# Four modulation units of layer 1 inside attention's last quarter, and experts 0 to 3 loaded ahead of the first gather

## What is computed

```python
def _ada(cond, w_ada, b_ada):
    m = (jax.nn.silu(cond) @ w_ada + b_ada)[..., None, :]
    return jnp.split(m, N_MOD, axis=-1)

for i in range(DEPTH):                      # once for the context, once for the latent tokens
    sh_a, sc_a, g_a, sh_f, sc_f, g_f = _ada(c, w_ada[i], b_ada[i])
    h = _modulate(x, sh_a, sc_a)            # layernorm(x) * (1 + scale) + shift
    ...                                     # attention (i = 0) or Fourier mixing (i = 1) -> out
    x = _post_norm(x, g_a * out, ln_gain[i, 0], ln_bias[i, 0])
    h = _modulate(x, sh_f, sc_f)
    moe = _hier_moe(h, ...)                 # top-1 group, top-2 experts in it, gated MLP
    x = _post_norm(x, g_f * moe, ln_gain[i, 1], ln_bias[i, 1])
```

## Time and profile before

| | |
|---|---|
| median of 3 runs | 989.13 us (987.59 to 990.61) |
| the profiled execution | 989.98 us, span in the trace 988.2 us |
| TensorE busy (matmuls) | 833.8 us, 84% |
| VectorE busy | 342.2 us, 35% |
| HBM read | 313.62 MB; mean 328 GB/s over the span |
| chain that ended last | TensorE 47%, DMA 32%, VectorE 13% |
| `DMA ring<-in_w_expert_up` in it | 17% |
| layer 0: first gather, first gate/up | 317.64 us, 326.94 us |

### The profile page before, as it was taken

The page is one execution under the profiler, slowest core; times in us unless marked ns, Lnnn a source line. Parts: engine busy times, 40 slices in busy tenths (PEclk is TensorE's granted clock), DMA queues, the critical chain, the costliest instruction groups (busy, mean ns, idle before and its releaser), DMA issues.

```text
span 988.2 us, 12750 instructions
## 1 busy us (share of the span) xinstructions
PE 833.8 (84%) x4891; PEld 428.5 (43%) x4891; DVE 342.2 (35%) x832; ACT 140.3 (14%) x327; POOL 164.5 (17%) x250
## 2 busy tenths in 40 slices
PE   3889999998898798998888788999599978786954
PEld 3555666665458333333333335547333323332311
DVE  2113454555587111111111138568511110111146
ACT  0122222223110111111101012001111100110110
POOL 1041212123111211111111100131201111111000
PEclk9989999999996999999899999998599998999978
DMA  9997393438449897999999979968999999999951
GB/s 335 366 358 289 114 380 126 170 131 324 156 126 415 353 402 285 420 420 418 419 419 418 417 284 370 350 234 298 351 383 419 418 419 418 419 420 419 417 194 64
DMA packets 91756, 324.54 MB, mean 328 GB/s; under 512 B 12654, under 2 KB 25678, under 8 KB 67608
## 3 DMA queue, kind: packets, MB, share of 16 engines
q1 hardware_dynamic: 73936, 287.84, 74.1%
q0 software_dynamic: 12704, 21.86, 6.3%
q10 hardware_dynamic: 5032, 13.71, 3.5%
HBM read 313.62 MB, written 32.05 MB: 350 GB/s over the span
## 4 chain that ended last, share of the span: by engine, by line
PE 47%; DMA 32%; DVE 13%; issue 4%; ACT 2%; POOL 2%; SPq 1%; POOLq 0%; ACTq 0%; DVEq 0%
DMA ring<-in_w_expert_up 17%; PE psum L1028 15%; PE psum L908 8%; DMA h_hT<-in_w_expert_up 5%; PE psum L1050 5%; PE psum L804 4%; PE psum L880 3%; DMA arena<-h_scratch,gidx 3%; PE psum L855 3%; DMA ring<-in_w_ada 3%; PE psum L1012 2%; DMA y_scratch<-arena,sidx 2%; DMA m_scratch<-m 1%; DMA ring<-y_scratch 1%; PE psum L959 1%
## 5 line engine op out<-in xcount | busy, mean ns | idle before, releaser
L1028 PE MATMUL psum<-ring,arena 128*64 128x512 f32 x880 | 260.3, 638 | 35.4 <-DMA ring<-in_w_expert_up 26.2
L1028 PEld LDWEIGHTS psum<-ring,arena 128*64 128x64 f32 x880 | 86.5, 146 | 168.9 <-issue 165.7
L1050 PE MATMUL psum<-ring,arena 128*64 128x512 f32 x440 | 124.1, 598 | 20.2 <-DVE arena L1809 19.6
L1805 DVE TENSOR_TENSOR arena<-arena,psum 128x256 f32<-128x256 f32 x34 | 14.3, 420 | 283.7 <-ACT arena L1363 283.7
L1028 PE MATMUL psum<-h_hT,arena 128*64 128x512 f32 x208 | 96.2, 617 | 7.2 <-DMA ring<-in_w_expert_up 6.3
L908 PE MATMUL psum<-ring,h_hT 128*128 128x384 f32 x288 | 98.1, 494 | 0.0
L855 PE MATMUL psum<-ring,h_hT 128*128 128x512 f32 x160 | 69.3, 593 | 1.8 <-ACT h_hT L1448 1.5
L908 PEld LDWEIGHTS psum<-ring,h_hT 128*128 128x128 f32 x288 | 54.4, 194 | 35.0 <-issue 1.6
L664 POOL DMA_INDIRECT y_scratch<-arena,sidx x32 | 32.6, 1019 | 208.4 <-DVE arena L1815 208.4
L804 PE MATMUL psum<-ring,silu 128*32 128x128 f32 x1536 | 55.2, 306 | 14.0 <-DMA ring<-in_w_ada 14.0
L1050 PEld LDWEIGHTS psum<-ring,arena 128*64 128x64 f32 x440 | 35.6, 136 | 71.6 <-issue 46.9
(11 more groups left out here) (215 smaller groups left out, 884.3 us busy)
## 6 DMA issues: line engine op xcount, KB each, us to landing
ring<-in_w_expert_down SPq DMA_DIRECT2D x52, 1024.0 KB, 21.4
ring<-in_w_expert_gate SPq DMA_DIRECT2D x50, 1024.0 KB, 19.0
ring<-in_w_expert_up SPq DMA_DIRECT2D x50, 1024.0 KB, 22.0
ring<-in_w_ada SPq DMA_DIRECT2D x24, 2048.0 KB, 14.6
h_hT<-in_w_expert_gate SPq DMA_DIRECT2D x12, 1024.0 KB
h_hT<-in_w_expert_up SPq DMA_DIRECT2D x12, 1024.0 KB
h_hT<-in_w_expert_down SPq DMA_DIRECT2D x12, 1024.0 KB, 26.6
ring<-in_w_qkv SPq DMA_DIRECT2D x9, 1024.0 KB, 12.6
```

The lines of the kernel that those rows point to most:

```text
L1028: last = pe.matmul(bank[b][64 * e:64 * e + 64, :].rearrange("p (g n) -> p g n", g=2), mem.GT[b][:, c, 64 * e:64 * e + 64], w, start=(c == ...
L1050: last = pe.matmul(bank[5 + half][64 * e:64 * e + 64, :], mem.actT[b][:, f, 64 * e:64 * e + 64], w[:, f, 512 * half:512 * half + 512], sta ...
```

## The change

Units (1, 2) and (1, 3) move from behind the router into attention's quarter 4, which now holds four units at the steps 1, 3, 4 and 5 (two before, at 1 and 4). They share a bank region, so each waits for VectorE's read of the one before. Unit (1, 5) moves from behind the table matmuls to behind (1, 4) and the router. Places change: units 4 and 5 now use C1 and A2, so A0 and A1 are free once attention's output is projected. SyncE loads expert 0 behind unit (1, 2); expert 2 and the gate part of expert 3 when that projection is done (where units 4 and 5 were loaded); expert 1 after unit (1, 4); the up and down parts of expert 3 after unit (1, 5). Experts 2 and 3 no longer wait for the first gathers; expert 4 does, as before. Nothing is computed that wasn't before, and nothing is left out.

```diff
-BETWEEN = {1: [(0, 4), (0, 5), (0, 6)], 2: [(0, 7), (0, 8), (0, 9)], 3: [(0, 10), (0, 11)], 4: [(1, 0), (1, 1)]}
-SPOTS = {1: (1, 3, 5), 2: (1, 3, 5), 3: (1, 4), 4: (1, 4)}
+BETWEEN = {1: [(0, 4), (0, 5), (0, 6)], 2: [(0, 7), (0, 8), (0, 9)], 3: [(0, 10), (0, 11)],
+           4: [(1, 0), (1, 1), (1, 2), (1, 3)]}
+SPOTS = {1: (1, 3, 5), 2: (1, 3, 5), 3: (1, 4), 4: (1, 3, 4, 5)}
...
-PLACE.update({("ada", 1, u): place for u, place in enumerate(("A2", "C1", "A2", "C1", "A0", "A1"))})
+PLACE.update({("ada", 1, u): place for u, place in enumerate(("A2", "C1", "A2", "C1", "C1", "A2"))})
...
-        ADA_AFTER = {(0, 1): (0, 2), (0, 3): (0, 1), (1, 1): (1, 0)}
+        ADA_AFTER = {(0, 1): (0, 2), (0, 3): (0, 1), (1, 1): (1, 0), (1, 2): (1, 1), (1, 3): (1, 2)}
...
             load("ada", 1, 0)
-            sp.wait_ge(qkv_ps, 18)
-            load_expert(0, 0)
             sp.wait_ge(qkv_ps, 24)
             load("ada", 1, 1)
-            for u in (2, 3):
-                after_ada(1, u - 2)
-                load("ada", 1, u)
+            after_ada(1, 0)
+            load("ada", 1, 2)
+            load_expert(0, 0)
+            after_ada(1, 1)
+            load("ada", 1, 3)
+            after_ada(1, 2)
+            load("ada", 1, 5)
+            after_ada(1, 3)
+            load("ada", 1, 4)
             sp.wait_ge(proj_ps, 6)
-            for u in (4, 5):
-                load("ada", 1, u)
-            after_ada(1, 3)
+            load_expert(0, 2)
+            load_part(0, 3, 0, "w_expert_gate")
+            after_ada(1, 4)
             load_expert(0, 1)
             after_ada(1, 5)
-            first_rows_fetched(0)
-            for e in (2, 3):
-                load_expert(0, e)
+            load_part(0, 3, 1, "w_expert_up")
+            load_down(0, 3)
             load_last_slot(0)
...
-                for u in ((2, 3, 4), (10,))[l]:
+                for u in ((4, 5), (10,))[l]:
                     ada(1, u)
...
-                if l == 0:
-                    ada(1, 5)
                 pe.wait_ge(table_done, 3 * l + 3)
...
-                for u in (range(2, 6), (11, 10))[l]:
+                for u in ((4, 5), (11, 10))[l]:
                     ada_add(1, u)
```

More of the change, by code:

```diff
@@ L388, in ada_out @@
             else:
-                at = [(4, 0), (4, 0), (1, 1), (1, 2), (1, 3), (7, 0), (2, 0), (5, 0), (5, 0), (3, 0), (1, 1), (1, 2)][u]
+                at = [(4, 0), (4, 0), (4, 0), (4, 0), (1, 1), (1, 2), (2, 0), (5, 0), (5, 0), (3, 0), (1, 1), (1, 2)][u]
             return bank[at[0]][:, P * at[1]:P * at[1] + P]
-        ADA_AFTER = {(0, 1): (0, 2), (0, 3): (0, 1), (1, 1): (1, 0)}
+        ADA_AFTER = {(0, 1): (0, 2), (0, 3): (0, 1), (1, 1): (1, 0), (1, 2): (1, 1), (1, 3): (1, 2)}
         ADA_AFTER.update({(0, u): (0, u - 1) for u in range(4, ADA_UNITS)})
@@ L421, in load_gate_up, with load_part @@
                 for part, name in enumerate(("w_expert_gate", "w_expert_up")):
-                    sp.dma_start(mem.slot(e)[:, part * 2 * D:(part + 1) * 2 * D],
-                                 A[name][l][e].rearrange("(p k) n -> p (k n)", p=P)).then_inc(landed[SLOT_OF[e]], 16)
+                    load_part(l, e, part, name)
+            def load_part(l, e, part, name):
+                sp.dma_start(mem.slot(e)[:, part * 2 * D:(part + 1) * 2 * D],
+                             A[name][l][e].rearrange("(p k) n -> p (k n)", p=P)).then_inc(landed[SLOT_OF[e]], 16)
             def load_down(l, e):
```

## The result

The changed kernel takes 1001.77 us (median of 4 runs, 1000.22 to 1003.87) against 988.84 us (987.59 to 990.61) for before: ratio 1.0126, 95% interval 1.0101 to 1.0151. It is slower, as forecast, but by 12.9 us and not by 7.25: it lies 1.3 us above the range. The profiled execution took 1000.94 us, its span is 999.1 us. In `mixer_to_experts` and behind, lines on TensorE are numbered 8 higher than before, those on VectorE 6 higher.

What follows compares the result with a forecast made beforehand. TensorE was taken to set the pace to 392 us, transfers to bound layer 0's experts after; 4.8 - 0.3 + 0.8 + 0.55 + 1.4 = +7.25 us on 989.13 gave 996.4 us, range 990.5 to 1000.5.

Steps and rivals of the forecast that it cites:

- first gather: First gather of layer 0's experts: lands later because the DMA queue drains 2.1 MB later; +1.4 us, bounds 0 and 3.0.
- unit at s = 3: Attention's quarter 4: the unit ahead of head 2's projection counts whole, since TensorE has no idle time there; +1.9 us.
- wait for unit 3's weights: Quarter 4, step 5: unit 3's load stands behind expert 0 and lands late; +2.1 us, bounds 0 and 5.5.
- unit at s = 5 and the head behind it: Quarter 4, ahead of head 4's projection: a 1.9 us unit, 1.07 us hidden by VectorE's softmax difference; +0.8 us.
- routing: Behind the router two units instead of three, but VectorE's one-hot sum sets the start of the position matmuls; -0.3 us.
- transposes: First transposes of gathered rows in layer 0, at clock 0.50 once the unit before them is gone; +0.8 us.
- gate/up of pair 0: Layer 0's first gate/up, slower at the low clock; +0.55 us, the middle of bounds 0 and 1.1.
- Head start worth nothing: Loading experts 2 and 3 ahead, 15.7 us of transfer, only lengthens idle DMA time before 393 us; 0 us gain.
- rival of 980.7 us: Rival: the 15.7 us of transfer done early shorten layer 0's transfer-bound stretch, giving 980.7 us; chance 0.07.
- Nothing behind absorbs it: After the first gate/up the whole +7.25 us remains: TensorE paces to 392 us, transfers take the same 168 us.
- a case to which the forecast gave 0.04: Rival: VectorE or DMA waits set the projection stage's end and swallow the delay; 989 to 991 us, chance 0.04.
- all upper bounds: Rival: wait 5.5, gather 3.0 and gate/up 1.1 all at their upper bounds; +12.8, 1002 us, chance 0.08.

Runs made afterwards that it cites:

- second profile of the changed kernel: The changed kernel measured and profiled once more with no edit, against before: 1004.43 us, ratio 1.0160.
- the kernel of both late: The changed kernel with expert 0 loaded behind unit 3's weights and experts 2 and 3 after the first gathers: 990.12 us, 1.0016 of before.

## Why the prediction was wrong in size

For the units and for the lost head start the mechanism held. The step that failed is the price of the early loads: 0 for the head start and +1.4 us for the first gather, where the stores and the gather beside them, and the clock behind the gather, cost about 10 us. It was hidden in part by an error the other way: the kernel with the units moved and the loads late is 1.0028 of before, 2.8 us, and not the 5.85 us that the sum has without the gather. The second failed step is that a wait of TensorE was priced at its own length. By the forecast's own steps, in the changed kernel's profile against that of before:

| step | forecast | measured |
|---|---|---|
| unit at s = 3 | +1.9 | +1.9 |
| wait for unit 3's weights | +2.1 (0 to 5.5) | +3.7 (3.41 idle) |
| unit at s = 5 and the head behind it | +0.8 | +2.85 |
| last head of quarter 4, low clock | not seen | +1.4 |
| routing | -0.3 | -1.1 |
| stores late, so the first gather issued late | not seen | +2.8 |
| first gather | +1.4 | +1.4 |
| transposes | +0.8 | +0.8 |
| gate/up of pair 0 | +0.55 (0 to 1.1) | +1.2 |
| from there to expert 9's issue | 0 | +1.7 |
| sum | +7.25 | +16.6 |

- **Head start worth nothing**: right in what it says of 389 us and of the rival of 980.7 us. The idle DMA time, the stretch that stayed as long, and the pair without second passes show it from both sides. But "I take 0 us of gain from it" left open what it costs, and that is the largest error of the case: the kernel with the late loads is 11.9 us faster.
- **First gather**, the step that failed: "Places A0 and A1 of units 4 and 5 were filled after the projection by 4.2 MB; now experts 2 and half of 3's gate/up, 4.2 MB too, stand there." Equal bytes were taken as equal load. I never asked whether the stores to `h_scratch`, which share the DMA engines, would become late: the units' 2 KB rows gave way to 8 KB rows, and the stores went from 10.3 to 18.0 us. Loads cut into 2 KB rows, and so issued more slowly, brought back 10.5. That the gather's own +1.4 us came out was in part luck: it took 7.3 us in before and 8.6 us in the same kernel without second passes, though nothing differs up to there. And before was contended already: beside an emptier queue it takes 4.6 us.
- **Wait for unit 3**: mechanism and place right, size 3.4 instead of 2.1, inside the bounds; putting expert 0 behind it removed it. From 225.35 us, the issue of unit 2, to 250.7 the queue of SyncE moved 8.25 MB and not the 7.35 of the sum: 0.9 MB of unit 5, issued behind unit 3 at 243.50 us, had gone through before unit 3 was whole.
- **What follows a wait**: the sum counted a wait as its own length. In quarter 4 the low clock added 0.97 us on the unit, 0.66 on the head behind it, and 1.0 to 1.5 on the last head in five of the eight profiles in which TensorE waited there. That the wait causes the first two is supported by the run that removed it; for the last head it is only argued, since in the second profile of the changed kernel that one took 1.98 us. Nor does a wait always bring it: one of 2.72 us did not.
- **Gate/up**: "I take the middle, 0.55" was the mis-sized term; the value of layer 1, 9.89 us, was the right one to take, and the idle-matmul runs show that the clock sets it. With a warm clock it is 7.09 us, so before, at 8.78, paid 1.7 us too.
- **"Nothing behind absorbs it"** held from expert 9's issue to the last gate/up of layer 0 within 0.1 us in this profile, while in the second that stretch was 1.9 us shorter. In the kernel of both late it is VectorE and not TensorE that sets the end of the stage behind the projection, a case to which the forecast gave 0.04; it swallows a gain of 2 us there, not the delay. The +1.7 us before expert 9's issue is a down at low clock (5.0 us from 392.03, 3.8 in before) and a longer wait for a gather. Layer 1 gave back 2.8 us in one profile and 0.5 in the other, with no cause that I tested.
- **The range**: its rule, the forecast plus half the way to all upper bounds, gives 996.4 + 2.8 = 999.2 us and not the 1000.5 that was stated; the result lies above both.

Open: why expert 0's place in the queue changed how fast the last store landed 60 us later was not tried, nor whether the stores would be as quick on another queue, nor what decides whether the clock falls in a wait of 2.6 us.

## What to carry to other kernels

A load that is moved earlier is not free when its gain is nil: list the small transfers of other queues in the stretch that it moves to (here stores and a gather on the critical path), and look at the rows of the loads as well as their bytes. Ask whether the transfer engines will be busy without a gap until the stretch that they bound; if some slow step of the compute drains the queue first, no head start survives it. And price a wait of TensorE at its length plus the slow pieces behind it; where the wait can't be removed, a few idle matmuls of the right length in it gave 4.4 us in the kernel before, while 80 where 30 fit made the changed kernel no faster.

## What the runs showed of the hardware

- A 1 MB store took 5.7 us (median of three) with no expert load beside it, 10.5 us beside loads in 2 KB rows that were issued over 12.5 us, 18.0 us beside 8 KB rows. In the last case the queues of the stores and of the loads moved 740 and 686 packets, not equal bytes.
- The same indirect gather took 4.6 us with an emptier queue and 8.5 to 9.9 us beside expert loads.
- The first gate/up took 7.09 us at clock 1.00; with 0.50 at its start it took 8.4 to 9.96 us, by when the clock rose within it.
- In or right behind a wait of 2.6 to 3.4 us the clock fell to 0.50 in seven profiles, and did not in one (2.72 us).
